# First out-projection in three fp32r products with operands split during the recurrence, and experts chosen in eight steps with three dummy products

## What is computed

```python
mix = jnp.concatenate([y_a, y_b], axis=-1)         # attention heads | gated delta rule heads
x = x + jnp.einsum('bse,ed->bsd', mix, w_out[l])   # the out-projection: 256x1024 by 1024x1024
h = rmsnorm(x, ffn_norm[l]).reshape(B * S, D)
y = hierarchical_moe(h, w_group[l], w_router[l], w_gate[l], w_up[l], w_down[l])
x = x + y.reshape(B, S, D)
...
# hierarchical_moe: softmax over 4 groups, the best group; in it a softmax over 8 experts,
# the best two, weights p_group * p / (p1 + p2); gated MLP experts 1024 -> 256 -> 1024
```

## Time and profile before

| what | value |
|---|---|
| median of three runs | 795.76 us (793.94 to 797.08) |
| the profiled execution | 796.86 us, its span 795.1 us |
| TensorE busy | 742.2 us, 93% |
| VectorE, ScalarE, GpSimd busy | 443.9, 321.3, 44.0 us |
| HBM read | 206.31 MB, 261 GB/s over the span |

### The profile page before, as it was taken

The page is one execution under the profiler, slowest core; times in us unless marked ns, Lnnn a source line. Parts: engine busy times, 40 slices in busy tenths (PEclk is TensorE's granted clock), DMA queues, the critical chain, the costliest instruction groups (busy, mean ns, idle before and its releaser), DMA issues. The chain is left out here.

```text
span 795.1 us, 13968 instructions
## 1 busy us (share of the span) xinstructions
PE 742.2 (93%) x5673; PEld 539.8 (68%) x5673; DVE 443.9 (56%) x772; ACT 321.3 (40%) x554; POOL 44.0 (6%) x39
## 2 busy tenths in 40 slices
PE   8999999899989999887876899999999999999998
PEld 5979976564646656544544587666548788888886
DVE  3899765544642331230330589688385865776665
ACT  4666433411432340340340664588432434343431
POOL 1000021001000000000000032301100000000000
PEclk9999999999999999998999999999999999999999
DMA  8894449988989999999999996610025445664201
GB/s 279 294 368 160 159 156 405 333 338 313 418 327 415 410 418 418 414 418 415 420 420 410 399 281 231 219 40 2 1 106 212 160 159 185 224 221 165 106 1 54
DMA packets 106387, 208.17 MB, mean 262 GB/s; under 512 B 7861, under 2 KB 55254, under 8 KB 98526
## 3 DMA queue, kind: packets, MB, share of 16 engines
q1 hardware_dynamic: 105406, 205.19, 68.8%
q10 hardware_dynamic: 864, 2.18, 0.8%
q0 software_dynamic: 64, 0.05, 0.0%
HBM read 206.31 MB, written 1.08 MB: 261 GB/s over the span
## 5 line engine op out<-in xcount | busy, mean ns | idle before, releaser
L2654 DVE TENSOR_TENSOR unit_parts<-ring,unit_parts 128x2048 fp32r<-128x2048 f32 x33 | 75.5, 2289 | 58.9 <-ACT unit_parts L1964 58.9
L1964 ACT ACTIVATE unit_parts<-ring 128x2048 fp32r<-128x2048 f32 x33 | 62.9, 1912 | 73.9 <-PE psa L1323 43.0
L1038 PE MATMUL psv<-ring,arena 128*32 128x256 f32 x960 | 60.9, 410 | 15.4 <-DMA ring<-in_w_up_dram 13.1
L1322 PE MATMUL psv<-column_parts,unit_parts 128*128 128x512 f32 (+1 forms) x192 | 65.5, 389 | 1.6 <-DVE arena L2742 1.4
L1322 PE MATMUL psa<-column_parts,unit_parts 128*128 128x512 f32 (+1 forms) x192 | 65.1, 388 | 0.0
L1038 PEld LDWEIGHTS psv<-ring,arena 128*32 128x32 f32 x960 | 34.2, 118 | 37.4 <-issue 22.6
L1323 PE MATMUL psv<-column_parts,unit_parts 128*128 128x256 f32 (+1 forms) x192 | 52.0, 271 | 0.0
L1323 PE MATMUL psa<-column_parts,unit_parts 128*128 128x256 f32 (+1 forms) x192 | 52.0, 271 | 0.0
L2785 POOL TENSOR_TENSOR small<-small,consts 128x2 f32<-128x2 f32 (+4 forms) x15 | 28.2, 1884 | 381.8 <-DVE small L2488 239.8
L1770 ACT ACTIVATE arena<-psv 128x256 f32<-128x256 f32 x8 | 3.1, 383 | 100.1 <-PE psv L1038 100.1
L1322 PEld LDWEIGHTS psv<-column_parts,unit_parts 128*128 128x128 f32 x192 | 36.1, 188 | 9.3 <-DVE unit_parts L2654 1.5
(11 more groups left out here) (441 smaller groups left out, 1688.7 us busy)
## 6 DMA issues: line engine op xcount, KB each, us to landing
ring<-in_w_gate_dram SPq DMA_DIRECT2D x43, 1024.0 KB, 9.3
ring<-in_w_up_dram SPq DMA_DIRECT2D x39, 1024.0 KB, 5.1
arena<-in_w_down_dram SPq DMA_DIRECT2D x32, 1024.0 KB
ring<-in_w_mod_dram SPq DMA_DIRECT2D x24, 1024.0 KB, 7.8
ring<-in_w_in_dram SPq DMA_DIRECT2D x23, 1024.0 KB, 10.0
ring<-in_w_down_dram SPq DMA_DIRECT2D x11, 1024.0 KB, 7.2
ring<-in_w_out_dram SPq DMA_DIRECT2D x8, 1024.0 KB, 8.0
arena<-in_w_in_dram SPq DMA_DIRECT2D x8, 512.0 KB, 16.3
```

The costliest lines, as they stand in the source:

```text
L1038: mm = pe.matmul(mG[32 * e:32 * e + 32, f0:f0 + FF], XT[:, k, 32 * e:32 * e + 32], w, start=(k == 0), stop=(k == KD - 1))
L1322: pe.matmul(both_parts(bank, t_0, t_1), hi, col_parts[:, :, k, t_0:t_1], start=(k == 0), stop=False)
L1964: act.activation(unit_parts[q % 3][:, 0, :], slot_of(NPRE + u_), ACT.Copy).then_inc(upper_done, 1)
L2654: vec.tensor_tensor(lo, slot_of(NPRE + at["mlp"] + 3 * n + kind), hi, ALU.subtract).then_inc(lower_done, 1)
```

## The change

The out-projection becomes 96 fp32r products (`split_product`) in place of 32 plain fp32 ones. Its operands are split by other engines while the recurrence runs: ScalarE writes four upper parts of w_out (`upper_out`) and two of mixT; GpSimd subtracts for w_out units 0, 2 and 3 and for mixT k 0 to 3 (`lower_out`), VectorE for unit 1 and for mixT k 4 to 7. The upper parts take room in the arena that other tiles had, so first place 5 and cw_ka are loaded after the out-projection. SyncE issues gate units 0 to 3 of pass 0 before it waits for `delta_out_done`. ScalarE evicts the turned heads, behind the squares of the context. The choice of experts uses a maximum of eight and a match and replace; the dummy products go from 12 to 3.

```diff
@@ -171,7 +171,10 @@
                        ("in2_upper1", 22056, [P, SLOT]), ("in2_upper0", 24736, [P, SLOT])),
                       (("in1_upper0", 0, [P, SLOT]), ("in1_upper2", 4096, [P, SLOT]), ("in1_upper4", 12288, [P, SLOT]),
                        ("in1_upper3", 16424, [P, SLOT]), ("row_parts", 18984, [P, 2, KD, T]),
-                       ("in1_upper1", 23088, [P, SLOT]), ("gate_parts", 25136, [P, 2, KD, 8]))):
+                       ("in1_upper1", 23088, [P, SLOT]), ("gate_parts", 25136, [P, 2, KD, 8])),
+                      (("out_upper1", 8192, [P, SLOT]), ("out_upper2", 10240, [P, SLOT]), ("out_upper3", 14376, [P, SLOT]),
+                       ("mix_upper1", 17952, [P, 4, T]), ("out_upper0", 20008, [P, SLOT]), ("mix_lower", 22312, [P, 8, T]),
+                       ("mix_upper0", 25760, [P, 4, T]))):
             end = 0
             with ExitStack() as place:
                 for name, first, shape in group:
...
-        sqc, sqx = ar(8192, NB, D), ar(22180, NB, D)
+        sqc, sqx = ar(24360, D), ar(22180, NB, D)
...
@@ -413,6 +419,12 @@
 
         out_banks = (PSA[0], PSA[1], PSA[2], PSX[0])
 
+        OUT_AT = in1_count(len(IN1) - 1)
+
+        def out_unit(n):
+
+            return [v.rearrange("p (k n) -> p k n", k=4) for v in (out_upper[n][:], ring_lower[:, (NPRE - 4 + n) % NS, :])]
+
         def mview(n):
             return ring[:, mslot[n], :] if n < NS else xslot[:, n - NS, :]
...
@@ -904,32 +917,36 @@
             at["delta"] = nv
             mod_sums(MOD_DELTA[2])
 
-            def project(units, m, k0, k1):
+            def project(m, k0, k1):
 
                 half, b = divmod(m, 2)
                 for k in range(k0, k1):
-                    mm = pe.matmul(out_banks[m][:], mixT[:, k, b * P:(b + 1) * P], units[k // 4][:, k % 4, :],
-                                   start=(k == 0), stop=(k == KD - 1))
+                    w = out_unit(2 * half + k // 4)
+                    rows_ = mix_upper[k // 4][:, k % 4, b * P:(b + 1) * P], mix_lower[:, k, b * P:(b + 1) * P]
+                    mm = split_product(out_banks[m][:], rows_, [w_[:, k % 4, :] for w_ in w], k == 0, k == KD - 1)
                 if k1 == KD:
                     mm.then_inc(out_sum_ready, 1)
 
             pe.wait_ge(a_free, na)
-            pe.wait_ge(moba_values_copied, MH // 2)
-            out_units = (unit(2), unit(2))
-            project(out_units[0], 0, 0, 4)
-            project(out_units[0], 1, 0, 4)
+            nu += 4
+            pe.wait_ge(out_lower_done, 2)
+            project(0, 0, 4)
+            project(1, 0, 4)
             pe.wait_ge(delta_out_done, 1)
+            at["heads turned"] = nv + 1
             for hp in range(2):
                 bank = v_bank()
                 for hh in range(2):
                     for b in range(NB):
                         mm = pe.transpose(bank[:, hh * T + b * P:hh * T + b * P + P], o[:, b, 2 * hp + hh, :], ident)
                 mm.then_inc(v_ready, 1)
-            project(out_units[1], 2, 0, 4)
-            pe.wait_ge(v_free, nv)
-            project(out_units[0], 0, 4, KD)
-            project(out_units[0], 1, 4, KD)
-            project(out_units[1], 2, 4, KD)
+            pe.wait_ge(out_lower_done, 3)
+            project(2, 0, 4)
+            pe.wait_ge(in1_lower_done, OUT_AT + 3)
+            project(0, 4, KD)
+            project(1, 4, KD)
+            pe.wait_ge(out_lower_done, 4)
+            project(2, 4, KD)
 
             def route(k0, k1):
...
@@ -943,7 +960,7 @@
             pe.wait_ge(out_sum_added, NB)
             for kp in range(2):
                 turn_pair(xres, kp, v_bank()).then_inc(v_ready, 1)
-            project(out_units[1], 3, 0, KD)
+            project(3, 0, KD)
             pe.wait_ge(v_free, nv)
             pe.wait_ge(out_sum_added, NB + 1)
             pe.wait_ge(route_gained, 1)
@@ -980,7 +997,7 @@
             turn_pair(hnc, 3, a_bank()).then_inc(a_ready, 1)
             at["context turned"] = na
             pe.wait_ge(out_sum_added, 2 * NB)
-            keep_busy(PSX[0], 12)
+            keep_busy(PSX[0], 3)
             sel = rt[:, 0:NB * NE].rearrange("p (b e) -> p b e", b=NB)
             pe.wait_ge(chosen_done, 1)
             bank = v_bank()
@@ -1428,30 +1445,31 @@
             sp.wait_ge(v_ready, at["scores"])
             load_expert_unit(sp, 10, 0)
             stream(NPRE - 4, NPRE)
+
+            def ring_place_free(n):
+                sp.wait_ge(*freed[NPRE - NS + n])
+
+            for n in range(4):
+                ring_place_free(n)
+                load_expert_unit(sp, n, 0)
             sp.wait_ge(delta_out_done, 1)
             load_expert_unit(sp, 8, 0)
             load_expert_unit(sp, 11, 0)
-            sp.dma_start(cw_ka, w_in2[:, 512:768].rearrange("(k p) n -> p k n", p=P)).then_inc(ctx_a_landed, 16)
 
             def ctx_columns(c0):
 
                 return w_in2[:, bass.ds(c0, CTX_W)].rearrange("(k p) n -> p k n", p=P)
 
-            def ring_place_free(n):
-                sp.wait_ge(*freed[NPRE - NS + n])
-
-            for n in range(4):
-                ring_place_free(n)
-                load_expert_unit(sp, n, 0)
-            sp.wait_ge(v_ready, at["delta"])
-            sp.wait_ge(delta_out_done, 1)
-            load_first_place(sp, 5)
             sp.wait_ge(v_ready, at["mod", MOD_LAST - 1])
             sp.wait_ge(s_pad2, 16)
+            sp.wait_ge(squares_done, 4)
             load_first_place(sp, 4)
             for n in first_places:
                 ring_place_free(n)
                 load_expert_unit(sp, n, EPG)
+            sp.wait_ge(out_sum_ready, 2 * NB)
+            load_first_place(sp, 5)
+            sp.dma_start(cw_ka, w_in2[:, 512:768].rearrange("(k p) n -> p k n", p=P)).then_inc(ctx_a_landed, 16)
             sp.wait_ge(logits_ready, 1)
             load_first_place(sp, 6)
@@ -1712,16 +1730,39 @@
                     x_moba(n // 2 - 1)
             x_moba(3)
 
+            def upper_out(n):
+
+                u_ = NPRE - 4 + n
+                act.wait_ge(unit_landed[u_ % NS], 16 * (u_ // NS + 1))
+                act.activation(out_upper[n][:], slot_of(u_), ACT.Copy).then_inc(in1_upper_done, 1)
+
+            act.wait_ge(moba_values_copied, MH // 2)
+            act.wait_ge(s_pad2, 16)
+            act.activation(mix_upper[0][:], mixT[:, 0:4, :], ACT.Copy).then_inc(in1_upper_done, 1)
             x_mod(MOD_DELTA[0])
+            upper_out(0)
             act.wait_ge(v_ready, at["S"])
             act.dma_start(ffn_bc, v("ffn_norm").broadcast_to((P, D))).then_inc(s_ffn_bc, 16)
-            for n in MOD_DELTA[1:]:
-                x_mod(n)
+            x_mod(MOD_DELTA[1])
+            act.wait_ge(v_free, at["R"])
+            upper_out(2)
+            act.wait_ge(v_ready, at["QS"])
+            upper_out(1)
+            x_mod(MOD_DELTA[2])
+            act.wait_ge(v_ready, at["Y"])
+            upper_out(3)
             act.wait_ge(v_ready, at["delta"])
             act.dma_start(hnc[:], v("ctx_2").rearrange("a (b p) d -> p (a b) d", p=P)).then_inc(s_ctx, 16)
             act.wait_ge(s_ctx, 16)
-            for b in range(NB):
-                act.activation(sqc[:, b, :], hnc[:, b, :], ACT.Square, accum_out=ss5[:, b:b + 1]).then_inc(squares_done, 1)
+            act.wait_ge(v_ready, at["mod", MOD_LAST - 1])
+            for b in range(NB):
+                act.wait_ge(squares_done, NB + b)
+                act.activation(sqc, hnc[:, b, :], ACT.Square, accum_out=ss5[:, b:b + 1]).then_inc(squares_done, 1)
+            for hp in range(2):
+                bank = PSV[(at["heads turned"] + hp - 1) % 3]
+                act.wait_ge(v_ready, at["heads turned"] + hp)
+                act.activation(mix_upper[1][:, 2 * hp:2 * hp + 2, :], bank[:].rearrange("p (h t) -> p h t", h=2), ACT.Copy,
+                               scale=vc[:, ROWS["gdn"]:ROWS["gdn"] + 1]).then_inc(in1_upper_done, 1)
 
             act.wait_ge(out_sum_added, 2 * NB)
             squares(xres, sqx)
@@ -2265,6 +2306,9 @@
             ov = o.rearrange("p b h j -> p (b h) j")
             dve.wait_ge(a_free, at["z"])
             link(vec.tensor_tensor(ov, ov, z.rearrange("p b (h j) -> p (b h) j", h=GH), ALU.mult))
+            dve.wait_ge(in1_upper_done, OUT_AT + 4)
+            vec.tensor_tensor(ring_lower[:, (NPRE - 3) % NS, :], slot_of(NPRE - 3), out_upper[1][:],
+                              ALU.subtract).then_inc(in1_lower_done, 1)
             dve.wait_ge(power_done, nrs)
             vec.tensor_tensor(ov, ov, spread(rsg, P), ALU.mult).then_inc(delta_out_done, 1)
             mod_cols(MOD_DELTA[2])
@@ -2274,8 +2318,12 @@
                                          vc[:, ROWS[name]:ROWS[name] + KD], ALU.add, ALU.mult)
             for hp in range(2):
                 bank = v_take()
-                vec.tensor_scalar(mixT[:, 4 + 2 * hp:6 + 2 * hp, :], bank[:].rearrange("p (h t) -> p h t", h=2),
-                                  vc[:, ROWS["gdn"]:ROWS["gdn"] + 1], None, ALU.mult).then_inc(v_free, 1)
```

(60 more changed lines are left out.)

44 lines of the change are left out of this document (15 added, 29 removed).

## The result

| what | before | after |
|---|---|---|
| median | 795.27 us (793.94 to 797.08, 4 runs) | 813.73 us (812.87 to 815.14, 4 runs) |
| the profiled execution | 796.86 us, its span 795.1 us | 813.56 us, its span 811.8 us |
| TensorE busy | 742.2 us, 93% | 739.5 us, 91% |

The ratio is 1.0232, 95% interval 1.0206 to 1.0258: 18.5 us slower. Forecast were 799.6 us, with a range from 791.0 to 802.5.

A forecast was written before the change was run, and what follows sets the result against it. Expert-weight transfers (399 to 420 GB/s) set the pace, with TensorE and the queue meeting at pass 2's gate weights. Out-projection end at 211.9 against 208.1 for no change gave 3.8 us later: median 799.6 us, range 791.0 to 802.5.

The forecast's parts named there:

- At no cost: Side effects priced at nothing: shorter tie constant, two VectorE memsets, one sqc buffer instead of two (0.2), lower parts in ring places.
- the sum for t4: Ahead of t4: GpSimd subtractions block VectorE, delta_out_done moves from 182.75 to 191.4, TensorE pauses 7.6 us; t4 becomes 211.9.
- t4: End of the out-projection, when VectorE adds its last bank: 205.4 us before the change, forecast 211.9.
- when the context lands: Second block's context, fetched by ScalarE after upper_out(3) ends at 178.9, lands between 184.9 and 187.4, taken as 187.
- Rival 1: VectorE goes first or is not blocked; the context's landing binds: t4 208.0, no change, 795.7 us; chance 0.25.
- Rivals 2 and 3: No blocking and context at 184.9: 791.8 us, chance 0.2; GpSimd's power also shuts VectorE out: 801.9 us, chance 0.1.
- from t4 to G2: Logits, expert choice and pass 0: up half starts at t4 + 18.1, pass 2's gate weights asked for at t4 + 39.9.
- G2: Issue of pass 2's gate weights by SyncE: 247.85 us before the change, forecast at t4 + 39.9.
- The 6.5 loads: Loads remaining at t4, claimed to take 16.6 us plus 1.3 to first bytes, so up-half weights bind at t4 + 17.9.
- the two meet: At pass 2's gate weights neither TensorE (248.85) nor the queue (249.0) has slack; delaying either delays the expert passes' end.

The follow-up runs named there:

- a_gap: The changed kernel plus an unused SBUF tile of 8 columns (32 bytes) behind the constants, restoring later tiles' places; 804.59 us, ratio to the kernel before 1.0119.
- b_gap: The kernel before plus an unused SBUF tile of 8 columns behind the constants, moving later tiles by 32 bytes; 806.16 us, ratio 1.0133.
- a_gap_short: `a_gap` with GpSimd's subtractions for w_out units 2 and 3 cut from 2048 to 8 columns, leaving out the product by their lower parts; 802.59 us.
- a_gap_dve: `a_gap` with VectorE instead of GpSimd subtracting for w_out units 2 and 3, nothing left out; 802.47 us.
- b_route: The kernel before plus an unused tile keeping places, with only the eight-step choice of experts and 3 dummy products; 797.59 us, ratio 1.0014.
- a_all_order: `a_gap_dve_evict` with SyncE loading first places 5, 6 and 7 ahead of pass 1's up units 6 and 7, cw_ka later; 794.54 us, ratio 0.9975.
- a_all_12: `a_gap_dve_evict` with 12 dummy products instead of 3; 794.64 us, ratio 0.9981.
- a_gap_dve_evict: `a_gap_dve` with ScalarE also evicting the turned heads before it waits for the second block's context; 797.93 us, ratio 1.0027.

## Why the prediction was wrong

It was wrong twice. The mechanism of its longest step was right, its close agreement in part luck.

**Not in it: the tiles' place.** Under "At no cost" I put the shorter tie constant. This is the first step that failed: it cost 9.1 us, half of the result (`a_gap`, `b_gap`). I had asked what the constant does and who reads it, not what lies behind it.

**Right in its mechanism: the sum for t4.** Without that, in `a_gap`, t4 is 212.20 where I had 211.9. Its terms one by one: GpSimd's subtractions 4.6 us (4.55, 4.57, 5.15 with its wait); squares of `o` held to GpSimd's end and 1.1 us behind; `lower_out(3)` first and the last scaling behind it, end 191.4 forecast, 190.6 measured; TensorE's pause 7.6 forecast, 7.1 measured; products at 0.23 each at full clock; the granted clock at the 1.2 GHz level behind the pause. From the end of the scaling to t4 I had 20.5 us and it was 21.6, most of it the clock: the transposes took 1.97 us in place of about 1.05, and the next ten products came 0.43 us apart, together about 2.9 where I had 2.0. So an error of 0.8 us one way and one of 1.1 the other leave the 0.3, which is luck.

That VectorE stands still for the whole rest of GpSimd's instruction was a guess from the other direction; `a_gap_short` shows it, with 1.22 and 1.22 us where `a_gap` has 4.17 and 5.52. The other order shows too: a GpSimd subtraction that started while VectorE's (2310) still ran took 5.15 us in place of 4.55. For the subtractions the trace so agrees, in both orders, with the rule of the Trainium skill, SBUF — State Buffer, section "Who interferes with whom" (whichever of the two comes first blocks the other fully). For GpSimd's power it does not: in the kernel after, unit 1's lower part started at 185.02, 1.1 us into the power (183.94 to 186.53), and took its usual 2.29 us.

**Right by luck: when the context lands.** I had it at 187, and in `a_gap` it was 188.1. But I had put its fetch behind upper_out(3), at 178.9, with 8.1 us to land:

```profile
175.35 0.39 ACTq L1756 DMA_DIRECT2D arena<-in_ctx_dram  x1
176.70 1.90 ACT L1738 ACTIVATE out_upper<-ring 128x2048 fp32r<-128x2048 f32 x1
188.11 1.06 ACT L1761 ACTIVATE arena<-arena 128x1024 f32<-128x1024 f32 x1 [9.51 <-DMA arena<-in_ctx_dram]
```

It was issued at 175.35, at the same time as before the change, while upper_out(3), which stands ahead of it in the program, only began at 176.70. The splitting on ScalarE did not delay the fetch at all. And it took 12.7 us, not 8.1, with four gate units issued ahead of it from 170.56 on. The two errors, 3.6 and 4.7 us, nearly cancel.

Rival 1 (the context binds) was the next bound and not a rival: it stood 2 us behind, as `a_gap_dve` shows. Rivals 2 and 3 are out: the context took 12 us, and the power did not shut VectorE out.

**Wrong: from t4 to G2.** The choice was right (TensorE turns to it at t4 + 8.0, the gate half ends at t4 + 17.2, in the kernel after, in `a_gap` and in `b_route`). This is the second step that failed: "the up half starts at t4 + 18.1, the gate weights of pass 2 are asked for at t4 + 39.9". In `a_gap` these are 21.1 and 44.6. Stretches of its trace:

```profile
187.00:191.00 4.00, 0.34 (x2) 0.35 (x3) 4.00 (x2) 2.30 (x4) 2.52 (x1) 0.50 0.00 1
201.00:203.00 2.00, 2.00 (x10) 1.62 (x9) 0.00 (x1) 0.00 (x0) 0.00 (x0) 1.00 0.00 0
210.00:213.00 3.00, 3.00 (x20) 2.61 (x18) 2.21 (x4) 0.08 (x1) 0.00 (x0) 1.00 0.00 0
213.00:220.00 7.00, 6.93 (x54) 5.63 (x53) 4.50 (x18) 6.81 (x13) 0.70 (x1) 1.00 0.95 335
220.00:232.00 12.00, 8.71 (x107) 6.82 (x106) 4.38 (x23) 3.74 (x6) 0.00 (x0) 1.00 1.03 399
255.00:257.00 2.00, 2.00 (x36) 1.17 (x29) 0.00 (x0) 0.00 (x0) 0.00 (x0) 1.00 0.01 2
```

The first three rows are stretches in which the queues stand empty while SyncE waits for places. The 6.5 loads were counted rightly, but I gave them the rate of the full stream, 2.55 us each from the first byte, and took the last byte as the landing. Their row starts in empty queues at 213, gets 335 and then 399 GB/s: 6.8 MB are through at about 231 (7 us at 335, 11 at 399), and TensorE goes on at 233.3. That is 3.0 us more. The other 1.7 us are the clock: I gave the half clock to the pause in the out-projection and forgot it at the pause that my own sum made (the gate half ends at t4 + 17.2, the up half starts later). The nine dummy products that the change took out had covered this wait.

**Half wrong: "the two meet".** TensorE's chain and the queues met at G2 before. In `a_gap` the queues are dry around 255 to 257 (2 GB/s), as a row above shows, before SyncE asks for more at 256.84: there TensorE alone sets G2. In `a_all_order` the queues do. That a delay of G2 is a delay of the end held well: `a_gap`'s passes end 8.9 us later with G2 9.0 later. So I add up: 0.3 at t4 and 4.7 behind it are the 5.0 us between 799.6 and 804.6, and 9.1 are the place.

## What to carry to other kernels

Where a wait is taken away or a constant is made shorter, look at what lies behind it: in memory too. Compare the rate of long transfers in a stretch that the change does not touch; if it moved, put the tiles back in place before anything else is measured. A dummy product, or a step of another engine, that ends just ahead of an event is not waste; ask first which wait it covers. Where two waits end within 2 us of each other, price them together: here one was worth 0.6 us or nothing, the other 2.1, and both 6.7. Where a term comes out right, check its parts too: the landing of the context was right by two errors of 4 us.

## What the runs showed of the hardware

- **The place of a tile in SBUF sets the rate of the transfers into it.** Shifts of all tiles by 32, 64 and 128 bytes cost 9.6 to 10.8 us (402 to 403 GB/s in the passes), by 256 and 512 bytes nothing (415). With only the arena shifted, loads into the ring kept their rate (404 against 384 GB/s). Why is not shown. Where the first tile starts is not known to me, so the runs fit a grid of 256 bytes and do not show the address that it is counted from.
- **VectorE stands still behind GpSimd.** A VectorE step with two SBUF inputs that came upon a GpSimd subtraction of 2048 columns waited for its whole rest, 5.26 and 5.52 us in place of 1.22. Beside a GpSimd power of 8 columns (2.59 us) it did not wait.
- **ScalarE's queue issues a transfer while its earlier work still stands in line.** The context's was issued at 175.35 in `a_gap`, ahead of an activation at 176.70 that comes before it in the program.
- **The same short pause sometimes costs 1.7 us and sometimes nothing.** The stage of the second block between two loads of SyncE takes 89.5 us in some traces and 87.8 in others, whatever the kernel. Before (first row) and in `a_all_12` (second and third), at and behind a pause of 1.9 us of TensorE:

```profile
590.00:600.00 10.00, 10.00 (x30) 5.07 (x31) 7.59 (x13) 1.50 (x4) 0.00 (x0) 0.83 0.52 200
```

```profile
580.00:590.00 10.00, 8.11 (x26) 3.94 (x25) 8.09 (x12) 1.53 (x4) 1.24 (x2) 1.00 0.21 63
590.00:600.00 10.00, 10.00 (x48) 6.36 (x46) 7.32 (x13) 2.27 (x6) 0.55 (x1) 1.00 0.61 214
```

The granted clock is 0.83 in the one and 1.00 in the other; why is not shown. The same happens ahead of the out-projection, at 150 to 165 us (0.89 in `a_all_order`, 1.00 before). So spans of single profiles differ by 1.7 us without a cause in the kernel, and I compared t4 and G2 within one trace. The profiled executions of `a_gap_dve`, `a_gap_dve_evict` and `a_all_order` lie 2.6 to 3.5 us above their medians.
